# Feed-forward pairs of a hybrid transformer block: seven products in another order over a ring of four PSUM banks

## What is computed

```
def gated_conv_ffn(x, w_gate, w_up, conv_w, conv_b, w_down):
    g = jnp.einsum('bsd,df->bsf', x, w_gate)
    g = causal_dwconv3(g, conv_w) + conv_b
    up = jnp.einsum('bsd,df->bsf', x, w_up)
    return jnp.einsum('bsf,fd->bsd', jax.nn.silu(g) * up, w_down)
```

## Time and profile before

| | us |
|---|---|
| median of 3 runs | 1763.34 (1761.65 to 1764.85) |
| profiled execution | 1763.92 |
| its span | 1762.2 |
| TensorE matmul busy | 1704.7 (97%) |
| TensorE weight load busy | 1483.7 (84%) |
| DVE busy | 1101.8 (63%) |
| ACT busy | 898.0 (51%) |
| POOL busy | 634.2 (36%) |
| line 2565, idle just before matmuls, by operand xs_u, xs_b | 19.3 and 8.5 |

### The profile page before, as it was taken

One profiled execution on the slowest core, in us unless ns is written; L12 is line 12 of the kernel. 1 busy time (PEld: TensorE's weight loads), 2 busy tenths in 40 slices (PEclk: granted clock), 3 DMA queues, 4 the chain that ended last, 5 costly groups with the idle time before them and its releaser, 6 DMA issues.

```text
span 1762.2 us, 29513 instructions
## 1 busy us (share of the span) xinstructions
PE 1704.7 (97%) x9907; PEld 1483.7 (84%) x9907; DVE 1101.8 (63%) x1967; ACT 898.0 (51%) x1685; POOL 634.2 (36%) x735
## 2 busy tenths in 40 slices
PE   7999999999999999999989999999999979999998
PEld 6788889999878888888869999888788879999887
DVE  6677767777763334674577888433356678887332
ACT  6666766666652233433456666322363556665222
POOL 4555665655520001000246666011004256665000
PEclk9999999999999999999989999999999999999999
DMA  4112123333323334133366666433232466665332
GB/s 137 52 46 62 51 60 74 74 85 78 78 72 95 95 108 129 51 93 102 110 143 140 148 150 132 128 99 102 86 95 72 124 138 152 143 151 118 99 98 90
DMA packets 298449, 178.83 MB, mean 101 GB/s; under 512 B 13967, under 2 KB 283154, under 8 KB 298354
## 3 DMA queue, kind: packets, MB, share of 16 engines
q1 hardware_dynamic: 281714, 148.69, 29.8%
q0 software_dynamic: 16448, 28.59, 10.1%
q10 hardware_dynamic: 192, 0.33, 0.1%
HBM read 147.02 MB, written 2.16 MB: 85 GB/s over the span
## 4 chain that ended last, share of the span: by engine, by line
PE 60%; DVE 15%; issue 9%; ACT 8%; POOL 5%; DMA 3%; DVEq 0%; ACTq 0%; POOLq 0%
PE ps L411 38%; PE ps L2565 5%; PE ps L1027 3%; DVE ps L2891 2%; PE ps L3054 2%; ACT w_split L2619 2%; PE ps L877 2%; DMA x_sum<-x_tok 1%; DVE w_split L2625 1%; POOL w_raw L2841 1%; POOL w_raw_b L2841 1%; DVE tmp L1370 1%; POOL w_split L2625 1%; DVE arena_r L1375 1%; PE ps L890 1%
## 5 line engine op out<-in xcount | busy, mean ns | idle before, releaser
L411 PE MATMUL ps<-arena_r,w_split 128*128 128x512 f32 x1854 | 425.2, 390 | 1.7 <-POOL w_split L366 1.5
L411 PEld LDWEIGHTS ps<-arena_r,w_split 128*128 128x128 f32 x1854 | 347.3, 188 | 76.9 <-POOL w_split L366 1.9
L411 PE MATMUL ps<-u,w_split 128*128 128x512 f32 x1641 | 400.5, 396 | 0.0
L352 ACT CAST w_split<-w_raw 128x1024 fp32r<-128x1024 f32 (+4 forms) x249 | 213.2, 874 | 306.2 <-PE ps L411 264.8
L368 DVE TENSOR_TENSOR w_split<-w_raw,w_split 128x1024 fp32r<-128x1024 f32 x149 | 179.2, 1203 | 297.5 <-ACT w_split L352 297.4
L411 PEld LDWEIGHTS ps<-u,w_split 128*128 128x128 f32 x1641 | 304.5, 189 | 63.3 <-issue 0.5
L2565 PE MATMUL ps<-xs_u,w_split 128*128 128x256 f32 x1728 | 226.9, 288 | 19.3 <-DVE w_split L2625 8.6
L2565 PEld LDWEIGHTS ps<-xs_u,w_split 128*128 128x128 f32 x1728 | 216.7, 195 | 24.9 <-issue 9.3
L1978 POOL TENSOR_TENSOR tmp<-tmp 128x512 f32<-128x512 f32 x33 | 46.7, 1415 | 261.2 <-ACT tmp L1934 232.5
L366 POOL TENSOR_TENSOR w_split<-w_raw,w_split 128x256 fp32r<-128x256 f32 x168 | 122.8, 762 | 23.8 <-ACT w_split L352 23.8
L1975 POOL COPY tmp<-tmp 128x512 f32<-128x512 f32 x5 | 3.2, 646 | 341.5 <-ACT tmp L1934 175.9
(11 more groups left out here) (335 smaller groups left out, 2761.7 us busy)
## 6 DMA issues: line engine op xcount, KB each, us to landing
w_raw<-in_w_in_dram SPq DMA_DIRECT2D x118, 256.0 KB, 3.2
w_raw<-in_w_ffn_down_dram SPq DMA_DIRECT2D x64, 256.0 KB, 3.1
w_raw<-in_w_ffn_gate_dram SPq DMA_DIRECT2D x52, 256.0 KB, 3.5
w_raw<-in_w_ffn_up_dram SPq DMA_DIRECT2D x52, 256.0 KB, 3.5
w_raw_b<-in_w_ffn_up_dram SPq DMA_DIRECT2D x36, 256.0 KB, 4.1
w_raw_b<-in_w_ffn_gate_dram SPq DMA_DIRECT2D x36, 256.0 KB, 3.6
w_raw_b<-w_raw_b POOLq DMA_DIRECT2D x36, 256.0 KB, 4.6
w_raw<-w_raw POOLq DMA_DIRECT2D x36, 256.0 KB, 3.8
```

The costliest lines, as they stand in the source:

```text
L352: ins = act.copy(dst, src)
L411: last = pe.matmul(out_ap, w_tile(c, ws, k - n0), moving(k, ms), start=start and n == 0, stop=stop and n == len(total) - 1, skip_group_che ...
```

## The change

`SEVEN` becomes p1, p2, p4, p3, p6, p5, p7, with p4 and p3 of the pair before at positions 2 and 3. The accumulating bank of a pair comes from a ring of four, 4, 5, 0, 1, and p1 waits for `hidden` of the pair four back. POOL's two low halves are now those of p1 and p2. `hidden` and the two halves of its result move one period back on ACT and DVE, to just ahead of `add_up_right` and behind p3's high half. `snap` of p1 moves on ACT ahead of the last plain tile's high part (`plain_hi`), and that goes behind the high half of p7. On POOL the third sum is issued before the fourth, and the fourth also waits for p2's low half. SP loads u1, u2, g1, g2. T3 is added to right behind T1N and T4 and counts a semaphore of its own (`x_third`); its splits go behind the first tap of the last plain tile. The load of the spatial biases counts the semaphore of the spatial weights.

```
-SEVEN = ("p1", "p4", "p3", "p2", "p6", "p5", "p7")
-OF_LAST = (1, 2)
+SEVEN = ("p1", "p2", "p4", "p3", "p6", "p5", "p7")
+OF_LAST = (2, 3)
...
-        R_BANK, T_BANK, Q_BANK, CONV_BANK = 4, 6, 7, 2
+        R_BANKS, T_BANK, Q_BANK, CONV_BANK = (4, 5, 0, 1), 6, 7, 2
+
+        def r_bank(gs):
+            return R_BANKS[(gs - PLAIN) % 4]
...
-            for name in ("u1", "g1", "u2", "g2"):
+            for name in ("u1", "u2", "g1", "g2"):
...
-                        low_split(sp, layer, i, gs - 1, 1 if name == "u2" else 2)
+                        low_split(sp, layer, i, gs - 1, OF_LAST[name == "g2"])
...
-                    pe.wait_ge(sem("ffn_a_done"), per_tile(layer, i, gs, 2))
+                    pe.wait_ge(sem("ffn_a_done"), per_tile(layer, i, gs, 4))
...
-            elif m == 4:
-                pool.wait_ge(sem("x_sum"), 48 * layer + 32)
...
             def fourth_sum(i, gs):
+                low_split(pool, layer, i, gs, 1)
                 low_split(pool, layer, i, gs, 4)
...
             pool_x_add(pool, layer, 0)
             pool_x_add(pool, layer, 1)
+            pool_x_add(pool, layer, 4)
             scaled(1)
             pool_x_add(pool, layer, 2)
             pool_x_add(pool, layer, 3)
             first_sum(0, PLAIN)
             third_sum(0, PLAIN)
-            pool_x_add(pool, layer, 4)
...
                 if fs < FT - 1:
                     first_sum(i, fs + 1)
+                    third_sum(i, fs + 1)
                 fourth_sum(i, fs)
-                if fs < FT - 1:
-                    third_sum(i, fs + 1)
...
                 begun, carried = fs < FT, fs > PLAIN
+                if fs > PLAIN + 1:
+                    hidden(i, fs - 2)
                 if carried:
                     add_up_right(i, fs - 1)
...
                 if carried:
                     add_gate_right(i, fs - 1)
                 if begun:
-                    lo_ahead(i, fs, 3)
-                    if not carried:
-                        dve_x(dve, layer, "p3")
+                    add_gate_left(i, fs)
```

More of the change, by code:

```diff
@@ L62 @@
 }
-SEVEN = ("p1", "p4", "p3", "p2", "p6", "p5", "p7")
-OF_LAST = (1, 2)
-ORDER = ([(PLAIN, p) for p in (0, 3, 4, 5, 6)] + [(f, p) for f in range(PLAIN + 1, FT) for p in range(7)]
+SEVEN = ("p1", "p2", "p4", "p3", "p6", "p5", "p7")
+OF_LAST = (2, 3)
+ORDER = ([(PLAIN, p) for p in range(7) if p not in OF_LAST] + [(f, p) for f in range(PLAIN + 1, FT) for p in range(7)]
          + [(FT, p) for p in OF_LAST])
@@ L2749, in snap @@
                 dst = {1: gpad[:, gs % 2, 2:2 + HT], 2: gpad[:, gs % 2, 2 + HT:2 + SEQ], 3: up2[:, gs % 2, :]}[which]
-                act.copy(dst, bank(R_BANK + gs % 2, 0, HT)).then_inc(sem("snap"), 1)
+                act.copy(dst, bank(r_bank(gs), 0, HT)).then_inc(sem("snap"), 1)
             def first_tap(i, gs):
@@ L2778, in period @@
                     act_seventh(act, layer, 0, *LAST_TWO[1])
+                hi_ahead(i, fs, 0)
+                if fs > PLAIN + 1:
+                    hidden_hi(i, fs - 2)
+                if fs == FT:
                     w_hi(act, c0 + 2 * PLAIN)
                 if begun:
-                    hi_ahead(i, fs, 0)
-                    if not carried:
-                        plain_hi(PLAIN - 1)
                     snap(i, fs, 1)
[L2785 to L2791, removed]
+                for pos in (1, 2, 3):
+                    hi_ahead(i, fs, pos)
+                if not carried:
+                    plain_hi(PLAIN - 1)
+                    act_x(act, layer, "p3")
+                hi_ahead(i, fs, 4)
                 if carried:
                     first_tap(i, fs - 1)
+                if begun:
+                    snap(i, fs, 2)
                 if fs == FT:
@@ L2796, in period @@
                     w_hi(act, c0 + 2 * PLAIN + 1)
[L2797 to L2804, removed]
+                hi_ahead(i, fs, 5)
+                hi_ahead(i, fs, 6)
                 if fs == FT - 1:
@@ L2860, in pool_ffn @@
             second_sum(0, PLAIN)
+            seventh_low(pool, layer, 0, *ORDER[1])
             scaled(3)
@@ L2945, in add_gate_left @@
                 dve.wait_ge(sem("snap"), snapped(layer, i, gs, 1))
-                dve.wait_ge(sem("s_used"), used(layer, i, gs, 3))
+                dve.wait_ge(sem("s_used"), used(layer, i, gs, 1))
                 left = gpad[:, gs % 2, 2:2 + HT]
@@ L2951, in add_gate_right @@
                 dve.wait_ge(sem("snap"), snapped(layer, i, gs, 2))
-                dve.wait_ge(sem("s_used"), used(layer, i, gs + 1, 2))
+                dve.wait_ge(sem("s_used"), used(layer, i, gs + 1, 3))
                 right = gpad[:, gs % 2, 2 + HT:2 + SEQ]
@@ L2957, in hidden @@
                 dve.wait_ge(sem("ffn_silu"), per_tile(layer, i, gs))
[L2958 removed]
+                dve.wait_ge(sem("s_used"), used(layer, i, gs + 1, 2))
                 dve.wait_ge(sem("combined"), combined(layer, i, gs, "up_right"))
[L2960 removed]
+                dve.scalar_tensor_tensor(out=bank(CONV_BANK + gs % 2), in0=bank(r_bank(gs)), scalar=-1.0,
                                          in1=cnv[:, gs % 2, :], op0=ALU.mult, op1=ALU.mult).then_inc(sem("ffn_a_done"), 1)
```

94 lines of the change are left out of this document (46 added, 48 removed).

## The result

The changed kernel took 1767.47 us (median of 12 runs, 1763.38 to 1770.7), the kernel before 1763.99 on the same chip (12 runs). The ratio is 1.0017, with a 95% interval of 1.0009 to 1.0025: no change by the bound of 0.2%, and if anything slower. 1736 with a range to 1752 had been predicted. Of two gains, one came as forecast and the other turned into a loss of almost the same size. The profiled execution took 1768.22 us; its span is 1766.5, 4.3 more than before.

What follows compares the result with a forecast made beforehand. TensorE, busy 97% of the span, was taken as the bound. Loop -19.1 and start -8.3 sum to -27.4 us, from 1763.92 profiled (0.6 above the median) to 1736 us; range 1727 to 1752.

Steps and rivals of the forecast that it cites:

- The start: First p1 of pair 4 to that of pair 5: T3's own semaphore and moved splits save 8.3 us over both layers.
- The end: Last pair: the stop of 1.02 us behind the last p7 stays; costed at zero.
- The loop: First product of pair 5 to last p7: runs at TensorE's pace, waits go, -19.1 us over both layers.
- p2's low half goes from DVE to POOL and p4's from POOL to DVE: the same number on each: Loop, swap of two low halves between engines, 0.67 and 1.29 us each: costed at nothing.
- SP issues that load now when p4's low half is done, about 0.2 us after p1's start: Loop, load ahead of POOL's first sum: this early issue leaves 0.3 us cover on ACT; costed at nothing.
- So this stop goes entirely: Loop, wait before p4: two products, 2.87 us, now cover a chain of 1.95 us, so no stop remains.
- covered, by 0.5 at least: Loop, p5 behind gate_right: DVE's work of 0.3 to 0.9 us fits within one product of 1.43 us.
- D: Rival, loop: DVE sets the pace, low halves slowed by POOL's sums; 24 us slower, 1788 us; chance 0.05.
- C: Rival: loop gains nothing, another wait (p5 behind gate_right) takes over, T3's queue eats the start; 1760 to 1767; chance 0.04.
- A: Rival, loop: adding DMAs set the pace, ACT waits before p3's high half; 0.3 us a period, 1747 us; chance 0.20.
- its terms 0.2, 3.1, 1.3 and 0.9: Loop, times from p1's start to issue of the fourth sum's DMA, given as 5.6 us; landing at 10.2.
- 169.1 + 0.4: Loop, per layer: 118 products at 1.433 us are 169.1 us, plus 0.4 given back for pair 5.

Runs made afterwards that it cites:

- yield_lock: Changed kernel plus one wait: GpSimd (POOL) holds the second sum until VectorE (DVE) has made p4's low half; 1746.37 us, kernel before 1760.81 beside it.
- yield_gate: Changed kernel plus GpSimd's wait for p4's low half before the second sum, and the gate_right addition ahead of p7's low half; 1738.86 us, kernel before 1760.81.
- gate_alone: Changed kernel with VectorE's gate_right addition moved ahead of p7's low half, as in the kernel before; 1764.31 us, kernel before 1760.81 beside it.
- hidden_after: Changed kernel with VectorE's addition for up_right ahead of the hidden product of the pair before, instead of behind it; 1769.10 us, kernel before 1762.25.
- sum2_half: Changed kernel with GpSimd's second sum cut to 256 of its 512 columns; 1753.31 us, kernel before 1761.92 beside it.
- low4_pool: Changed kernel with p4's low half back on GpSimd and p2's on VectorE; 1757.72 us, kernel before 1762.25 beside it.

## Why the prediction was wrong

**The start** was right. Forecast for layer 0: p1 910.8, p2 914.4, p6 915.9, p5 919.0, p7 922.1, next p1 923.8. Measured: 911.25, 914.84, 916.38, 919.31, 922.36, 923.89. The gain forecast for the two starts from the old place of p1 was 8.3 us (4.3 and 4.0). Measured it is 4.2 in layer 0 and 5.2 in layer 1 (5.75 shorter, begun 0.54 later behind the layer before), and the clock held.

**The end** was as forecast: the stop ahead of the last p4 is 1.10 us, 1.02 before.

**The loop** failed: -19.1 us forecast, +13.0 measured. The step that failed is "p2's low half goes from DVE to POOL and p4's from POOL to DVE: the same number on each", costed as "Nothing". The instructions and their own lengths balance, but the two low halves are not alike. p4's is the one that SP's load of u2 waits for, and on DVE it can be held off by whatever POOL has next, which is the second sum. The same mistake stands once more further on: "SP issues that load now when p4's low half is done, about 0.2 us after p1's start". In a period of 10.02 us that is true (the load of the fast period before 978 is issued 0.3 after p1). In the slow ones it is 2.2 (1056.48 against 1054.29), and all the cover behind it is gone. I had taken 0.67 for this low half where it took 2.64. "So this stop goes entirely" (at p4) was right only in the fast periods, for the same reason.

A second step failed beside it: for p5 behind gate_right, with one more low half in front, the prediction had "covered, by 0.5 at least". TensorE waits there for 14.2 us in all, partly for the ring. What this place costs is the difference of yield_lock and yield_gate, which differ in it alone: 347.1 and 340.1 us for both loops, 7.1 us. The wait on POOL comes first: 371.1 us in the changed kernel, 347.1 in yield_lock, 24.0 us.

**The rivals.** D had the mechanism, low halves on DVE standing off behind POOL, and the wrong question: it asked whether DVE as a whole runs out of time, which needs all five low halves at 1.36. One of them at 2.64 is enough if it lies on a ring, and DVE is idle 31 us in the loop while it happens. The page "SBUF — State Buffer" of the Trainium skill, "Who interferes with whom", was cited there for the lock itself; the runs agree with it (1.42 us behind one instruction of POOL, 0.68 to 0.72 alone). C had named the place (p5 behind gate_right) and came nearest in time, 1760 to 1767, for a cause that gate_alone excludes. A did not happen: in the slow periods ACT does wait for the fourth sum's DMA before p3's high half (1.19 us at 1056.18), but TensorE goes through p3 without a stop. A's price was also off by its own terms, since a DMA 1 us later over a cover of 0.3 is 0.7 us late and not 0.3; and its terms 0.2, 3.1, 1.3 and 0.9 add up to 5.5, not 5.6.

**The forecast's own terms** come out in yield_gate: 169.29 us in the loop of layer 0 against 169.1 + 0.4, and 18.1 us less over both loops where 19.1 were forecast. In all it took 1738.86 us against 1736 forecast; the kernel before took 1760.81 beside it, so the gain by medians is 22.0 us and not 27.4. Most of what was forecast for the order of products and the four banks is there. What was missing is one wait on POOL, and the place of one addition.

What stays open: why the loop of the changed kernel runs at 10.02 at first and then turns over to 11.2. Both are stable as seen, and the late p4 of one period makes the next one late; which small delay turns it was not found. That POOL's next instruction goes first is shown by the rows in which it happens. One time in the rows goes with the outcome (last section), but no run changed it alone.

## What to carry to other kernels

Swapping two equal instructions between two engines is not free: ask of each what waits for it, and what can get in front of it on the new engine. A chain that leads from an instruction through a load and sums back to the same instruction one period on is a second clock of the loop; add it up for the changed order and compare it with the period of the bounding engine. Where VectorE and GpSimd hold each other off, decide the order with a wait: holding the instruction that is not urgent back until the urgent one is done made this kernel faster by 0.9%. Put additions on which the next product hangs ahead of work that has three products of time.

## What the runs showed of the hardware

- A low half on DVE that is issued while POOL works waits not only for that instruction: 1053.81 (DVE) is older than 1054.39 (POOL's second sum), and the second sum is through first. With two of POOL's in front it took 2.63 and 2.64 us, with one 1.42 (yield_lock), alone 0.68 to 0.72. In gate_alone, issued earlier still, it took 3.25. The page "SBUF — State Buffer" of the Trainium skill, "Who interferes with whom", says that DVE and GpSimd contend by an exclusive lock and that the order of issue decides who blocks. The wait for the instruction in flight agrees with it. Where both wait for the same instruction of POOL, the recorded starts do not: DVE's stood there 0.58 us longer than the second sum and went behind it.
- Which of the two goes first goes together with one time in the rows. The changed kernel has 34 places where a low half of DVE is still open when POOL ends the low half ahead of its second sum. In 22 of them the second sum's recorded start lies 0.21 us or more before that end, and DVE waits for the second sum too (2.17 to 2.85 us). In the 12 others it lies at most 0.05 before that end, or behind it, and DVE goes first (0.69 to 1.98 us; the fast period of 978 is one of these). gate_alone and hidden_after divide in the same way, all 64 places, with 0.16 as the least of the first kind and 0.08 as the most of the second; sum2_half has one exception in 33. In 18 of the 22 the second sum starts 0.13 us behind the landing of the adding DMA that it needs; whether a later landing would keep the loop at 10.02 us was not tested. All this is an association: no run moved that start alone.
- The same program keeps a pace for many periods: in the changed kernel 10.02 us in the first part of the loop of layer 0, and 11.0 to 11.3 after it and in nearly all of layer 1.
- The clock of TensorE fell to its lower level behind a stop of 2.17 us in layer 0 (950.30, the stretch ahead at 1.00), held behind one of 2.34 us in layer 1 of the same kernel, and held in the start through stops of 1.90, 1.33 and 1.37 us. The loops of low4_pool had three falls and one stop of 2.17 us without; the starts of hidden_after had falls behind stops of 1.89 and 1.90. What decides it could not be told from the rows. Behind the stops of 2.17 us in low4_pool p5 and p7 take 4.47 us with a fall and 2.96 without, so a fall costs 1.5 us there; in the starts of hidden_after it cost nothing.
